# Output projection of a hybrid attention block: sums of merged tiles made by accumulating transfers within SBUF, with signs moved, a first product that waits by halves, and four output rows

## The reference, cut to what matters

```python
y_a = jnp.einsum('bse,ed->bsd', o_a, w_up_a)
y_b = jnp.einsum('bse,ed->bsd', o_b, w_up_b)
merged = jax.nn.sigmoid(mg_a) * y_a + jax.nn.sigmoid(mg_b) * y_b
sub = jnp.einsum('bsd,de->bse', merged, w_out)
return layer_norm(DEEPNORM_ALPHA * x + sub, ln_g, ln_b)
```

## Time and profile before

| what | value |
|---|---|
| time before, median of 3 runs | 719.07 us (718.83 to 720.89) |
| profiled execution, time | 718.53 us |
| its span, first to last instruction | 716.7 us |
| granted TensorE clock, mean | 0.994 |
| TensorE busy | 695.8 us, 97% |
| VectorE busy | 580.1 us, 81% |
| ScalarE busy | 457.6 us, 64% |
| GpSimd busy | 123.5 us, 17% |

### The profile page before, as it was taken

How to read it: one execution, slowest core, us unless ns; L and a number is a source line. 1 busy time by engine, 2 the same in 40 slices (tenths; PEclk the granted TensorE clock), 3 DMA queues, 4 the chain that set the end, 5 groups by cost and what they waited for, 6 DMA issues and landing times.

```text
span 716.7 us, 10825 instructions
## 1 busy us (share of the span) xinstructions
PE 695.8 (97%) x3926; PEld 565.8 (79%) x3926; DVE 580.1 (81%) x791; ACT 457.6 (64%) x793; POOL 123.5 (17%) x146
## 2 busy tenths in 40 slices
PE   8999999999999999999999999999999999999992
PEld 6788877777888788788888888888888788777772
DVE  6999788765998987898899774567779877899986
ACT  7954477776866866777587774565579655753632
POOL 0000000000553323232232310000000000000497
PEclk9999999999999999999999999999999999999997
DMA  8336332231669745350113214666345866775123
GB/s 295 117 86 132 107 94 85 74 94 44 230 204 205 210 115 121 67 141 16 45 30 101 84 52 132 203 242 216 100 137 162 265 217 172 263 272 208 58 89 117
DMA packets 54884, 100.34 MB, mean 140 GB/s; under 512 B 12816, under 2 KB 17424, under 8 KB 54544
## 3 DMA queue, kind: packets, MB, share of 16 engines
q1 hardware_dynamic: 48912, 82.88, 35.6%
q0 software_dynamic: 5920, 16.78, 10.1%
HBM read 78.67 MB, written 35.65 MB: 160 GB/s over the span
## 4 chain that ended last, share of the span: by engine, by line
PE 82%; DVE 7%; POOL 5%; issue 3%; ACT 2%; DMA 1%; SPq 1%; DVEq 0%; POOLq 0%; ACTq 0%
PE ps L255 22%; PE ps L257 21%; PE ps L256 21%; PE ps L2191 5%; PE ps L2203 5%; PE ps L2176 4%; POOL o_t L937 3%; POOL o_t L939 2%; DVE t_ops L1782 1%; PE ps L2120 1%; PE ps L2132 1%; PE ps L2101 1%; DVE x_lo L1782 1%; DMA raw<-in_w 1%; DVE keep L1712 1%
## 5 line engine op out<-in xcount | busy, mean ns | idle before, releaser
L255 PE MATMUL ps<-x_hi,w_hi 128*128 128x512 f32 x432 | 173.7, 402 | 1.1 <-DVE x_lo L1619 0.9
L257 PE MATMUL ps<-x_hi,w_lo 128*128 128x512 f32 x432 | 168.8, 391 | 0.0
L256 PE MATMUL ps<-x_lo,w_hi 128*128 128x512 f32 x432 | 168.4, 390 | 0.0
L1504 DVE TENSOR_TENSOR w_lo<-raw,w_hi 128x512 fp32r<-128x512 f32 x142 | 96.6, 693 | 53.2 <-ACT w_hi L965 52.7
L255 PE MATMUL ps<-t_ops,w_hi 128*128 128x512 f32 x288 | 115.1, 400 | 0.3 <-issue 0.3
L257 PE MATMUL ps<-t_ops,w_lo 128*128 128x512 f32 x288 | 112.5, 390 | 0.0
L256 PE MATMUL ps<-t_ops,w_hi 128*128 128x512 f32 x288 | 112.3, 390 | 0.0
L1712 DVE TENSOR_TENSOR_SCAN keep<-keep 128x895 f32<-128x895 f32 (+4 forms) x64 | 86.1, 1376 | 14.9 <-POOL keep L872 14.9
L255 PEld LDWEIGHTS ps<-x_hi,w_hi 128*128 128x128 f32 x432 | 81.2, 188 | 18.7 <-issue 3.5
L257 PEld LDWEIGHTS ps<-x_hi,w_lo 128*128 128x128 f32 x432 | 81.1, 188 | 17.5
L256 PEld LDWEIGHTS ps<-x_lo,w_hi 128*128 128x128 f32 x432 | 81.4, 188 | 15.2
(11 more groups left out here) (236 smaller groups left out, 1181.8 us busy)
## 6 DMA issues: line engine op xcount, KB each, us to landing
raw<-in_w SPq DMA_DIRECT2D x51, 256.0 KB, 3.0
raw<-in_w SPq DMA_DIRECT2D x20, 512.0 KB, 3.9
sig_m<-sig_d SPq DMA_DIRECT2D x16, 512.0 KB, 4.6
sig_d<-sig_m SPq DMA_DIRECT2D x28, 256.0 KB, 2.7
up_sum_d<-in_w POOLq DMA_DIRECT2D x6, 1024.0 KB, 10.1
out_sum_t_d<-in_w POOLq DMA_DIRECT2D x6, 1024.0 KB, 10.0
xr<-in_xt SPq DMA_DIRECT2D x16, 256.0 KB, 5.7
o_t<-o_d SPq DMA_DIRECT2D x8, 512.0 KB, 4.6
```

The lines of the kernel that those rows point to most:

```text
L255: pe.matmul(out, w_hi, x_hi, start=first, stop=False, skip_group_check=goes_on)
L256: pe.matmul(out, w_hi, x_lo, start=False, stop=False, skip_group_check=goes_on)
L257: return pe.matmul(out, w_lo, x_hi, start=False, stop=last, skip_group_check=goes_on)
L1504: dve.tensor_tensor(ring_slot(w_lo, q), part_of(q), ring_slot(w_hi, q).bitcast(F32), ALU.subtract).then_inc(part_lo, 1)
```

## The change

It does seven things.

1. `out_sum` is gone from VectorE. After its attention work GpSimd issues eleven transfers, SBUF to SBUF, of which eight accumulate. For s2: copy A11, add A21 (1 MB each), add the two halves of A22 (0.5 MB each). For s1: copy A21, add A22. For s4: three adds in place into A12's quarter (A11, A21, A22). For s3: copy A11, add A21. All but the first of each start behind a wait for the one before to have landed, on two counters (`wo_summed` for s2, `up_summed` for the rest), so that s1's add, the three of s4 and the two of s3 form one chain. The first waits for 166 products of the up projection (`LAST_UP + 5`), the halves of A22 for 12 and 15 merged tiles, s1's copy for all 168 products, s4's first add also for A12's low part, s3's copy also for the four groups of product 1.
2. Since these transfers only add, signs move: the merged tiles of the second half of channels (`j >= UP_PAIRS // 2`) are written negated, t2 is split negated (`NEGATED`), the copy of product 1 in PSUM is negated, and some additions of `c11` and the like turn into subtractions and the reverse. The number of these instructions stays the same.
3. ScalarE and VectorE wait for s2, s1, s4 and s3 on the transfer counters; the order of the split is now t2, t1, s2, s1, t3, B22, s4, s3, A22, t4.
4. s2 and t2, and A22 and t4, swap their slots (2 and 6), and SyncE's load of t2 stands one product later.
5. The first group of product 1 waits for the first halves of A11 and B11, and for the rest ahead of its third step of `k`.
6. Output rows: GpSimd and VectorE write `o_t[:, s % 4]`, so row s waits for the store of row s - 4, on four counters.
7. GpSimd waits for the whole of s3 (`sums_done(7)`) ahead of its first row of the layer norm.

The diff, cut to its core:

```diff
-OUT_SLOT = {"A11": 1, "B11": 0, "B21": 5, "A12": 4, "s2": 2, "t2": 6, "s1": RING_SLOT, "t1": 3, "s4": 4, "B22": 5,
-            "s3": 1, "t3": 0, "t4": 6, "A22": 2}
+OUT_SLOT = {"A11": 1, "B11": 0, "B21": 5, "A12": 4, "s2": 6, "t2": 2, "s1": RING_SLOT, "t1": 3, "s4": 4, "B22": 5,
+            "s3": 1, "t3": 0, "t4": 2, "A22": 6}
@@ SyncE
-                elif q == LAST_UP + 5:
+                elif q == LAST_UP + 6:
                     load_out("t2")
-                    sp.dma_start(out[s][:, half(h)], o_t[:, 2 + s % 2, half(h)]).then_inc(out_done[s % 2], 16)
+                    sp.dma_start(out[s][:, half(h)], o_t[:, s % 4, half(h)]).then_inc(out_done[s % 4][0], 16)
@@ GpSimd
+            q11, q12, q21, q22 = (quarter(o_t, kh, nh) for nh in range(2) for kh in range(2))
+            low, high = slice(0, 2), slice(2, 4)
+            at_2, at_1, at_3 = out_room("s2"), out_room("s1"), out_room("s3")
...
+            pool.wait_ge(m_set, 8)
+            pool.wait_ge(product_done, LAST_UP + 5)
+            pool.dma_start(at_2, q11).then_inc(wo_summed[0], 16)
+            pool.wait_ge(*s2_done(1))
+            pool.dma_start(at_2, q21, accum_op=ALU.add).then_inc(wo_summed[0], 16)
+            pool.wait_ge(m_set, 12)
+            pool.wait_ge(*s2_done(2))
+            pool.dma_start(at_2[:, low], q22[:, low], accum_op=ALU.add).then_inc(wo_summed[0], 16)
+            pool.wait_ge(product_done, ALL_PRODUCTS)
+            pool.dma_start(at_1, q21).then_inc(up_summed, 16)
+            pool.wait_ge(m_set, 15)
+            pool.wait_ge(*s2_done(3))
+            pool.dma_start(at_2[:, high], q22[:, high], accum_op=ALU.add).then_inc(wo_summed[0], 16)
+            pool.wait_ge(*sums_done(1))
+            pool.dma_start(at_1, q22, accum_op=ALU.add).then_inc(up_summed, 16)
+            pool.wait_ge(wo_lo, out_ready("A12"))
+            pool.wait_ge(*sums_done(2))
+            pool.dma_start(q12, q11, accum_op=ALU.add).then_inc(up_summed, 16)
+            pool.wait_ge(*sums_done(3))
+            pool.dma_start(q12, q21, accum_op=ALU.add).then_inc(up_summed, 16)
+            pool.wait_ge(*sums_done(4))
+            pool.dma_start(q12, q22, accum_op=ALU.add).then_inc(up_summed, 16)
+            pool.wait_ge(wo_done, out_made(1, GROUP - 1))
+            pool.wait_ge(*sums_done(5))
+            pool.dma_start(at_3, q11).then_inc(up_summed, 16)
+            pool.wait_ge(*sums_done(6))
+            pool.dma_start(at_3, q21, accum_op=ALU.add).then_inc(up_summed, 16)
+            pool.wait_ge(*sums_done(7))
             pool.wait_ge(ln_in, 32)
             for s in range(SB - 1):
-                if s >= 2:
-                    pool.wait_ge(out_done[s % 2], 32 * (s // 2))
+                if s >= 4:
+                    pool.wait_ge(*counted(out_done[s % 4], 32))
@@ ScalarE
-                    act.wait_ge(*counted(s_set, out_summed(name, p)))
+                    if name == "s2":
+                        act.wait_ge(*counted(wo_summed, 16 * 12))
+                    else:
+                        act.wait_ge(up_summed, 16 * (8 + {"s1": 2, "s4": 5, "s3": 7}[name]))
             copy_first(0)
             copy_first(1)
             out_hi("A12", 2)
+            both_hi("t2")
             copy_first(2)
             copy_first(3)
+            both_hi("t1")
             both_hi("s2")
-            both_hi("t2")
             both_hi("s1")
-            both_hi("t1")
+            both_hi("t3")
+            both_hi("B22")
             both_hi("s4")
-            both_hi("B22")
             both_hi("s3")
-            both_hi("t3")
-            both_hi("t4")
             both_hi("A22")
+            both_hi("t4")
@@ VectorE
+                if j < UP_PAIRS // 2:
+                    dve.tensor_tensor(merged_at, o[:, 0, :], o[:, 1, :], ALU.add).then_inc(m_set, 1)
+                else:
+                    dve.scalar_tensor_tensor(out=merged_at, in0=o[:, 0, :], scalar=-1.0, in1=o[:, 1, :],
+                                             op0=ALU.mult, op1=ALU.subtract).then_inc(m_set, 1)
...
             out_lo("A12", 2)
-            for name in ("s1", "s2", "s4"):
-                out_sum(name, 0)
-                out_sum(name, 1)
+            both_lo("t2")
+            both_lo("t1")
             both_lo("s2")
-            both_lo("t2")
             both_lo("s1")
             c11(0)
-            out_lo("t1", 0)
             c11(1)
-            out_lo("t1", 1)
             c11(2)
+            c11(3)
+            both_lo("t3")
             c12_first(0)
-            c11(3)
-            both_lo("s4")
             c12_first(1)
             both_lo("B22")
             c12_first(2)
+            both_lo("s4")
             c12_first(3)
-            out_sum("s3", 0)
-            out_sum("s3", 1)
             c22_first(0)
             both_lo("s3")
             c22_first(1)
-            out_lo("t3", 0)
+            both_lo("A22")
             dve.wait_ge(ln_in, 32)
             row_done(0)
@@ TensorE
-                    pe.wait_ge(wo_lo, max(out_ready(s_name), out_ready(t_name)))
+                    pe.wait_ge(wo_lo, max(out_split(s_name, 0), out_split(t_name, 0)) if n == 1 and i == 0 else
+                               max(out_ready(s_name), out_ready(t_name)))
...
                 for k in range(4):
+                    if n == 1 and i == 0 and k == 2:
+                        pe.wait_ge(wo_lo, max(out_ready(s_name), out_ready(t_name)))
```

More of the change, by code:

```diff
@@ L232, in out_split @@
 def out_split(name, p):
-    return sum(len(out_pieces(n)) for n in SPLIT_ORDER[:SPLIT_ORDER.index(name)]) + p + 1
+    return SPLIT_ORDER.index((name, p)) + 1
 def out_ready(name):
     return out_split(name, len(out_pieces(name)) - 1)
-def out_summed(name, p):
-    return 2 * OUT_SUMS.index(name) + p + 1
 def out_made(n, i):
@@ L556, in build @@
         xn_in = [sem(f"xn_in{i}") for i in range(2)]
-        out_done = [sem(f"out_done{i}") for i in range(2)]
         masks, eps_set, ones_set, sink_set = sem("masks"), sem("eps_set"), sem("ones_set"), sem("sink_set")
@@ L848, in store_last @@
                     sp.wait_ge(ln_last, h + 1)
-                    sp.dma_start(out[SB - 1][:, half(h)], o_t[:, 2 + (SB - 1) % 2, half(h)]).then_inc(out_done[(SB - 1) % 2], 16)
+                    sp.dma_start(out[SB - 1][:, half(h)], o_t[:, (SB - 1) % 4, half(h)]).then_inc(out_done[(SB - 1) % 4][0], 16)
             for s in range(SB - 1):
@@ L853, in _ @@
             store_last()
-            sp.wait_ge(out_done[0], 32 * (SB // 2))
-            sp.wait_ge(out_done[1], 32 * (SB // 2))
+            for s in range(4):
+                sp.wait_ge(*counted(out_done[s], 32 * (SB // 4)))
         @block.gpsimd
@@ L934, in _ @@
                 for h in range(2):
-                    y = o_t[:, 2 + s % 2, half(h)]
+                    y = o_t[:, s % 4, half(h)]
                     pool.wait_ge(ln_norm, 2 * s + h + 1)
@@ L1568, in merge @@
                 dve.wait_ge(ol_done, 10 if j == 0 else 2 * NP)
-                dve.tensor_tensor(o_t[:, 2 * j + m, half(nh)], o[:, 0, :], o[:, 1, :], ALU.add).then_inc(m_set, 1)
+                merged_at = o_t[:, 2 * j + m, half(nh)]
+                if j < UP_PAIRS // 2:
[3 more added lines that the diff above has]
+                                             op0=ALU.mult, op1=ALU.subtract).then_inc(m_set, 1)
             def after(q):
@@ L1777, in out_lo @@
                 dve.wait_ge(wo_hi, out_split(name, p))
-                if name == "s2":
-                    dve.wait_ge(*counted(s_set, out_summed("s4", p)))
-                elif name == "s1":
-                    dve.wait_ge(*counted(s_set, out_summed("s2", p)))
-                dve.tensor_tensor(lo[:, at, :], out_source(name)[:, at, :], hi[:, at, :].bitcast(F32),
-                                  ALU.subtract).then_inc(wo_lo, 1)
+                if name == NEGATED:
+                    dve.scalar_tensor_tensor(out=lo[:, at, :], in0=out_source(name)[:, at, :], scalar=-1.0,
+                                             in1=hi[:, at, :].bitcast(F32), op0=ALU.mult,
+                                             op1=ALU.subtract).then_inc(wo_lo, 1)
+                else:
+                    dve.tensor_tensor(lo[:, at, :], out_source(name)[:, at, :], hi[:, at, :].bitcast(F32),
+                                      ALU.subtract).then_inc(wo_lo, 1)
             def both_lo(name):
@@ L1977, in _ @@
             s = SB - 1
-            y, st = o_t[:, 2 + s % 2, :], small[:, s % 2, :]
-            dve.wait_ge(out_done[s % 2], 32 * (s // 2))
+            y, st = o_t[:, s % 4, :], small[:, s % 2, :]
+            dve.wait_ge(*counted(out_done[s % 4], 32))
             dve.wait_ge(ln_var, SB)
```

62 lines of the change are left out of this document (24 added, 38 removed), and 3 rows, old and new, of the table SPLIT_ORDER.

## The result

| what | before | after |
|---|---|---|
| time, median | 718.95 us (718.78 to 720.89, 4 runs) | 763.47 us (762.53 to 764.69, 4 runs) |
| ratio to before, 95% interval | | 1.0618 (1.0604 to 1.0631) |
| profiled execution, its span | 718.53, 716.7 us | 763.64, 761.9 us |
| granted TensorE clock, mean | 0.994 | 0.966 |

The changed kernel is 44.5 us slower. I had forecast slower, but 735 us, and a range of 719 to 748 that does not hold the result.

A forecast was written before the change was run, and what follows sets the result against it. TensorE, 97% busy, and GpSimd's row operations in the tail were taken as bounds. GpSimd's start +18.8, its shorter run -1.8 and the free last row -1.1 gave 735 us, range 719 to 748.

The forecast's parts named there:

- the sign: Whole kernel: slower with chance 0.84, faster 0.14, same 0.02.
- the price of one accumulation: GpSimd's 1 MB accumulating transfers within SBUF: 8.0 us each with nothing beside them, 11.0 beside loads, as between DRAM tiles.
- The stall ahead of product 6: TensorE idles some 6 us there because s2 is ready at about 646; costs nothing in the sum.
- s1 whole at 652.0: GpSimd's transfers for s2 and s1, with SyncE's loads counted at half, 4 us, end at 652.0 us.
- s4 in 24 us: s4's three accumulations in place, one behind the other, take 24 us, to 676.0.
- GpSimd starts when s3 has landed: GpSimd's layer norm stands behind s3's transfers and starts at 690.8 instead of 671.97, 18.8 us later.
- The other path: TensorE from group (3,0) at 680.5 to 722.1, then row 7's tail of 8.5 us: end at 730.6, ahead of GpSimd's 732.6.
- the four output rows: At the end, row 7 waits for row 3's store, so VectorE's 2.86 us wait goes; 1.1 us gained.
- The halves: Product 1 waits for first halves, so TensorE's idle 0.88 us ahead of it goes.
- C: Rival, slower but less: accumulations 8.0 us each, loads beside them free; time 725 us; chance 0.18.
- D: Rival, slower still: every accumulation takes 11.0 us, from colliding loads or late descriptors; 15 us later, 750; chance 0.08.
- A: Rival, faster: an accumulation within SBUF costs little more than a 5.5 us copy, loads don't slow it; 711 us; chance 0.12.

The follow-up runs named there:

- a_light: The changed kernel with residual rows, gain and bias loaded only as 32-column slivers, 5 MB of SyncE's loads gone: 752.82 us, ratio to the kernel before 1.0469.
- a_copies: The changed kernel with every accumulating transfer turned into a plain copy of the same size: 742.95 us, ratio to the kernel before 1.0333.
- a_early: The changed kernel with steps for groups (3,1), (3,2) and row 0 moved ahead of the splits of s3 and A22 on VectorE and ScalarE: 767.52 us.
- b_rows4: The kernel before with the four output rows alone: 719.70 us against 718.79, ratio 1.0011.

## Why the prediction was wrong, step by step

**Right: the sign, the mechanism, the price of one accumulation.** I took 8.0 us from DRAM transfers for one within SBUF with nothing beside it; measured 7.9, 8.4 and 8.6. The largest stall is the one ahead of group (3,0), s4's low part, and the other predicted one stands ahead of product 6. The 0.88 us ahead of product 1 is gone, the signs cost nothing, VectorE's wait for a store is gone, GpSimd's 28 operations took 37.7 us (I took 39), and the low clock behind each long stall cost 1.5 to 1.8 us (I took 2.7, once). VectorE is no longer full. The stall ahead of product 6 I had right in its place and not in its size: some 6 us forecast, 18.36 measured, since s2 was whole at 659.4 and not near 646.

**Wrong by 15.5 us: s1 whole at 652.0, measured 667.5.** This is the term of the sum that was mis-sized, and in three places: s2's copy began 1.3 later and took 7.3 from start to next issue instead of 5.5 (3.1 in all), the first addition took 14.7 instead of 11.0 (3.7), the stretch behind it 27.9 instead of 19.2 (8.7). The cause is one. I took a landing time from a row with half a megabyte beside it for a transfer with 3.5 MB beside it; then I counted SyncE's loads at half their engine time; and I left out the block B22 and the layer norm's gain and bias, 2 MB that SyncE issues at 644.6 to 645.6. The engines were full for 42 us, and then a megabyte counts whole or nearly so. a_light shows it for the loads (10.5 us of them gone, s1 8.5 earlier), a_copies for the additions.

**Wrong by 4.0 us: s4 in 24 us, measured 28.0.** The first and the third addition took 8.4 and 7.9 and, with what lies between landing and issue, 8.7 and 8.5; the second took 10.6, beside a load of 1 MB that SyncE issued at 675.5. s3's copy and addition took 14.0 with what lies between them, 0.8 less than the 14.8 I had.

**Wrong by 10.8 us: GpSimd starts when s3 has landed.** It landed at 709.5; GpSimd began at 720.29. VectorE's timeline of the changed kernel has the cause:

```profile
710.64 2.36 DVE L1835 TENSOR_TENSOR x_lo<-wo_x,x_hi 128x1024 fp32r<-128x1024 f32 x2 [10.94 <-ACT x_hi L1408]
712.91 0.68 DVE L1869 SCALAR_TENSOR_TENSOR sig_m<-sig_m,ps 128x512 f32<-128x512 f32 x1
713.51 2.36 DVE L1835 TENSOR_TENSOR t_ops<-o_t,t_ops 128x1024 fp32r<-128x1024 f32 x2
715.78 0.68 DVE L1861 TENSOR_TENSOR raw<-raw,ps 128x512 f32<-128x512 f32 x1
```

VectorE works in its written order. It waited 10.94 us for s3's split while `c22_first(1)`, for which group (3,1) waits, and row 0 stood ready behind it: the third stall, 6.49 us. Row 0's statistics began at 716.38, ScalarE's scaling of it at 719.30, and only then had GpSimd something to do. I had asked who waits behind s4's split and not who waits behind s3's. That this queue is the cause of the third stall is shown by a_early, where the stall is gone and GpSimd starts 11.4 us earlier; that undoing it alone would have saved the time is refuted by the same run.

**The sum.** GpSimd's start is 15.5 + 4.0 - 0.8 + 10.8 = 29.5 us later than predicted (720.29 against 690.8), its run 1.3 shorter, and the end behind it 1.1 longer (3.9 instead of 2.8, row 7's stores behind row 6's on SyncE, as in b_rows4): 29.3 us of span, 761.9 against 732.6.

**The other path came out as late, and I had it 2 us earlier.** I put the end by TensorE and row 7 at 730.6. The profile's chain that ended last runs over this path, over the third stall, TensorE and row 7; VectorE's last row in the changed kernel:

```profile
756.89 1.63 DVE L2015 SCALAR_TENSOR_TENSOR o_t<-o_t,small,sig_m 128x512 f32<-128x512 f32 x1
```

Row 7 is finished at 758.5, half a microsecond behind GpSimd's 757.98. Group (3,0) started at 699.84 instead of 680.5, 19.3 late by the same two terms; from there TensorE took 49.9 us instead of 41.6, the third stall and the fourth with the low clock; and the tail was 12.2 instead of 8.5, in part because row 7's four multiply-adds took 6.2 us beside GpSimd, as in b_rows4. So the sum above accounts for GpSimd's path, but the end hangs on both, and an earlier start of GpSimd alone would have saved little.

**Wrong, and small: the four output rows.** I had them at a gain of 1.1 us; alone they cost 0.9. I had named the wait that goes, and not what it kept apart. The halves I credited with 0.88 us; in the kernel before they are worth nothing. Neither entered the sum of the changed kernel beyond the 1.1. Two slips of the text are smaller still: the 1.6 us of the earlier trace rows are two idle stretches and not one, and C counts 37.5 us for GpSimd's operations where the forecast counts 39.

**The rivals.** D, 750 us, was the nearest, but its mechanism, 11.0 us for every accumulation, is not what happened: where nothing ran beside them they took 8. D's other cause, descriptors that GpSimd writes late beside VectorE, is at most a small part: the DMA engines were not left idle from 617.6 to 659.4, and s4's additions took 8.4 us with VectorE busy 8.38 of 8.6 us and 7.9 with VectorE idle. A is refuted on both counts: where little ran beside them additions took 7.9 to 8.6 us and not 5.5, and beside the loads even copies took longer (a_copies). The range was too narrow above because its upper end came from a rival with one price for all places, and no case in it had the engines full for 40 us.

What stays open: how much of the 24 us that a_copies keeps is the issue and landing of eleven transfers, most of them one behind the other (2.9 us each by the earlier trace rows), how much the loads beside them, and how much the new order of splits. I ran no kernel that takes these apart.

## What to carry to other kernels

Before work moves from a compute engine to transfers, add up the engine time of everything that is queued in that stretch, plain bytes at one rate and accumulating bytes at about twice the time (here 2.6 and 5.1 to 5.5 us per MB); if the sum fills the stretch, a transfer's landing time from a quiet place says nothing. Move only the sum whose result is needed long after its operands are ready, one or two transfers of it (here s3 alone paid: 1.7 us gained), and put the wait for it on in-order engines behind everything that is ready earlier. A wait that one removes may have kept two engines out of each other's way, and a wait that one adds delays all that is queued behind it.

## What the runs showed of the hardware

- An accumulation of 1 MB within SBUF takes what one within DRAM takes: 7.9 to 8.6 us from issue to landing with little beside it (8.0 in the earlier trace rows), against 5.0 for a copy. In the middle of s4's last addition, alone, the engines were full (share 1.12) at 191 GB/s, 5.5 us per MB, against 206 within DRAM. *DMA: Bandwidth & Descriptors*, "Anatomy of one DMA — SWDGE (gpsimd) path", in the Trainium skill gives 2.0 us plus bytes by 436 GB/s, an estimate of 4.4 us. The copies are near it, the accumulations are not; the measurement decides.
- On full engines a load is slowed like the accumulations: the residual load that took 11.4 us before took 18.3, and the layer norm's bias 20.0 instead of 7.4.
- The granted clock was 0.50 (1.2 GHz) in the stretch from 698 to 702 us, which holds the first matmuls behind the stall, 0.82 from 702 to 706 and 1.00 from 706 on. Behind each of the three long stalls six to eight matmuls came 0.42 us or more behind the one before instead of 0.227, and 1.5 to 1.8 us were lost a stall. Behind a_early's stall of 9.42 us it was thirteen.
- GpSimd's elementwise work beside VectorE's costs both: a pair of 128x1024 on VectorE 4.55 us instead of 2.35, an operation of 128x512 on GpSimd 2.1 to 2.2 instead of 1.29.
